# Chunked delta rule inside a four-mixer decoder trunk: values' products moved into the recurrence, panel chunks moved out of it

## What is computed

```python
def step(state, inp):
    qd, kd, uu, ww, aqk, gl = inp
    v_new = uu - jnp.einsum('bhcd,bhde->bhce', ww, state)
    o = jnp.einsum('bhcd,bhde->bhce', qd, state) + jnp.einsum('bhce,bhef->bhcf', aqk, v_new)
    state = state * gl[..., None, None] + jnp.einsum('bhcd,bhce->bhde', kd, v_new)
    return state, o
```

## Time and profile before

| | us |
|---|---|
| median of 3 runs | 2355.43 |
| lowest and highest | 2352.8, 2355.49 |
| the profiled execution's own time | 2352.03 |
| its span, first to last instruction | 2350.3 |

### The profile page before, as it was taken

The page is one execution under the profiler, slowest core; times in us unless marked ns, Lnnn a source line. Parts: engine busy times, 40 slices in busy tenths (PEclk is TensorE's granted clock), DMA queues, the critical chain, the costliest instruction groups (busy, mean ns, idle before and its releaser), DMA issues.

```text
span 2350.3 us, 37000 instructions
## 1 busy us (share of the span) xinstructions
PE 2318.3 (99%) x14463; PEld 2013.9 (86%) x14463; DVE 1434.4 (61%) x1556; ACT 1054.0 (45%) x1354; POOL 247.3 (11%) x254
## 2 busy tenths in 40 slices
PE   8999989999999999999999999999999999999999
PEld 7898878888888888888989899887888888888887
DVE  6664557555555555568666767565755554554556
ACT  4455454434434434435544445345443443443442
POOL 0052001000000000000032322200100000000000
PEclk9999999999999999999999999999999999999999
DMA  6663456665665665665534435354656656566564
GB/s 238 194 171 121 147 199 197 197 194 183 197 193 184 196 193 184 197 207 153 183 106 139 132 109 162 106 190 144 198 195 192 186 195 192 187 194 228 188 195 136
DMA packets 236680, 417.21 MB, mean 178 GB/s; under 512 B 23761, under 2 KB 46570, under 8 KB 234986
## 3 DMA queue, kind: packets, MB, share of 16 engines
q1 hardware_dynamic: 235162, 410.73, 55.5%
q10 hardware_dynamic: 1360, 4.19, 0.5%
HBM read 412.77 MB, written 2.10 MB: 177 GB/s over the span
## 4 chain that ended last, share of the span: by engine, by line
PE 95%; DVE 2%; issue 1%; ACT 1%; DMA 1%; POOL 0%; ACTq 0%; POOLq 0%; DVEq 0%
PE quad L643 20%; PE quad L668 13%; PE quad L670 13%; PE quad L669 13%; PE quad L646 10%; PE quad L614 5%; PE quad L616 5%; PE quad L618 5%; PE quad L721 1%; PE quad L1121 1%; PE quad L885 1%; PE quad L883 1%; PE quad L884 1%; PE quad L811 1%; DMA raw<-in_w_out 1%
## 5 line engine op out<-in xcount | busy, mean ns | idle before, releaser
L1684 DVE TENSOR_TENSOR wlo<-raw,whi 128x1024 fp32r<-128x1024 f32 x760 | 984.4, 1303 | 695.5 <-ACT whi L1264 692.4
L1264 ACT ACTIVATE whi<-raw 128x1024 fp32r<-128x1024 f32 x760 | 800.6, 1058 | 885.0 <-PE quad L670 468.5
L643 PE MATMUL quad<-xs,whi 128*128 128x512 f32 x2048 | 648.4, 397 | 5.4 <-DVE xs L2005 5.0
L668 PE MATMUL quad<-whi,hh 128*128 128x512 f32 x1248 | 488.7, 392 | 1.2 <-POOL hl L2373 1.0
L670 PE MATMUL quad<-whi,hl 128*128 128x512 f32 x1248 | 485.8, 389 | 0.0
L669 PE MATMUL quad<-wlo,hh 128*128 128x512 f32 x1248 | 485.6, 389 | 0.0
L646 PEld LDWEIGHTS quad<-xs,wlo 128*128 128x128 f32 x2048 | 386.2, 189 | 90.9
L646 PE MATMUL quad<-xs,wlo 128*128 128x256 f32 x2048 | 403.3, 278 | 0.0
L643 PEld LDWEIGHTS quad<-xs,whi 128*128 128x128 f32 x2048 | 314.0, 189 | 7.1 <-issue 5.8
L668 PEld LDWEIGHTS quad<-whi,hh 128*128 128x128 f32 x1248 | 234.3, 188 | 49.7 <-POOL hl L2373 1.4
L670 PEld LDWEIGHTS quad<-whi,hl 128*128 128x128 f32 x1248 | 234.2, 188 | 49.3
(11 more groups left out here) (325 smaller groups left out, 2112.5 us busy)
## 6 DMA issues: line engine op xcount, KB each, us to landing
raw<-in_mlp_w SPq DMA_DIRECT2D x512, 512.0 KB
raw<-in_gdn_w_in SPq DMA_DIRECT2D x105, 512.0 KB
raw<-in_w_out SPq DMA_DIRECT2D x64, 512.0 KB
raw<-in_mem_w_kv SPq DMA_DIRECT2D x32, 512.0 KB
raw<-in_mla_w_in SPq DMA_DIRECT2D x25, 512.0 KB
raw<-in_mla_w_ukv SPq DMA_DIRECT2D x24, 256.0 KB
gb<-in_ln_g SPq DMA_DIRECT2D x4, 1024.0 KB, 7.3
gb<-in_ln_b SPq DMA_DIRECT2D x4, 1024.0 KB, 9.4
```

Source lines behind the costliest of these rows:

```text
L643: last = nc.tensor.matmul(both, b.whi[:, slot, k, cols], b.xs[:, :, kt, :], start=start, stop=stop, skip_group_check=True)
L668: nc.tensor.matmul(ps[:, t, 0:n], ah[:, kt, toks], hi[:, k, 0:n], start=start, stop=False)
L1264: nc.scalar.activation(b.whi[:, c % NSPLIT], b.raw[:, slot], ACT.Copy).then_inc(sem.hi_ready, 1)
L1684: nc.vector.tensor_tensor(b.wlo[:, c % NSPLIT], b.raw[:, c % NRAW], b.whi[:, c % NSPLIT].bitcast(F32), ALU.subtract).then_inc(sem.lo_ready, 1)
```

## The change

- The values' product is no longer made for both halves ahead of the recurrence and copied to `uu`. A new function `new_values(g, j)` makes it for one chunk: four matmuls of 64x64 weights by 128 columns, written to those rows of the chunk's own bank in which L1185's correction comes to lie. For j = 0 it stands ahead of the keys' product; for j > 0 behind the previous chunk's output product, with `start=True`, and the state's product then accumulates onto it with `start=False`. The buffer `uu` and the signals `p_u` and `d_u` go.
- `vn` is now a plain copy from the bank: its first half on DVE, its second half (for j > 0) on ACT, with a signal of its own, `a_vn`. For j = 0 DVE copies both halves.
- The three `beside` calls inside the recurrence go; the seven chunks with indices 9 to 15 now follow it in a row. The `feed` calls inside the recurrence on ACT (three) and DVE (two) move behind it.
- The keys' products of the two chunk halves change banks, ACT copies those of the odd chunks first, and the first state increment goes to `side_ps[1]`, since the banks are needed by the accumulating products.
- PE begins chunk 0 without waiting for ACT's `wq` copies. ACT copies chunk j-1's output after its half of chunk j's `vn`.

```diff
 def out_half(j, upper):
-    c = j % 2 if j == 0 else 1 - j % 2
-    return half_rows(1 - c if upper else c)
+    return half_rows(j % 2 if upper else 1 - j % 2)
+
+def new_half(j, upper):
+    return half_rows(1 - j % 2 if upper else j % 2)
...
+            def state_bank(j):
+                return turn_ps[1] if j else side_ps[1]
...
                 for t in tiles:
                     pe.wait_ge(sem.d_xt, (g + 1) * (LEVELS - 1) * TT - TT + t + 1)
                     pe.wait_ge(sem.kd_set, g + 1)
+                    if t == 0:
+                        new_values(g, 0, True).then_inc(sem.p_vn, 1)
                     for h in range(GH):
                         for c in range(2):
                             r = slice(CHUNK * c, CHUNK * (c + 1))
-                            last = nc.tensor.matmul(turn_ps[c][:, (t * GH + h) * CHUNK:(t * GH + h + 1) * CHUNK], b.kb[r, t, h, :],
+                            last = nc.tensor.matmul(turn_ps[1 - c][:, (t * GH + h) * CHUNK:(t * GH + h + 1) * CHUNK], b.kb[r, t, h, :],
                                                     b.xt[r, t, h, :], start=t == 0 and h == 0, stop=True, skip_group_check=True)
                     last.then_inc(sem.p_w, 1)
-                    for h in range(GH):
-                        for c in range(2):
-                            r = slice(CHUNK * c, CHUNK * (c + 1))
-                            last = nc.tensor.matmul(side_ps[t][r, h * P:(h + 1) * P], b.xt[r, t, h, :], b.vr[r, t, h, :],
-                                                    start=h == 0, stop=True, skip_group_check=True)
-                    last.then_inc(sem.p_u, 1)
-                for t in tiles:
-                    pe.wait_ge(sem.a_w, n0 + t + 1)
                 for j in range(NC):
...
                     if j:
+                        pe.wait_ge(sem.a_w, n0 + 1)
+                        if j == 2:
+                            pe.wait_ge(sem.d_s, g * (NC - 1) + 1)
+                        if j == NC - 1:
+                            pe.wait_ge(sem.a_o, g * NC + 1)
+                        new_values(g, j, False)
                         pe.wait_ge(sem.d_s, g * (NC - 1) + j)
                         if j == 2:
-                            pe.wait_ge(sem.d_u, n0 + 2)
-                        if j == NC - 1:
-                            pe.wait_ge(sem.a_o, g * NC + 1)
+                            pe.wait_ge(sem.a_w, n0 + 2)
                         each(lambda h, o, s_: nc.tensor.matmul(o, b.wq[:, t, h, 2 * c:2 * c + 2, :].rearrange("p a i -> p (a i)"),
-                                                               state[:, h, :], start=s_, stop=False, skip_group_check=True),
+                                                               state[:, h, :], start=False, stop=False, skip_group_check=True),
                              bank, sem.p_vn)
-                        beside(g, LEAD + LEVELS - 2 + j)
                     pe.wait_ge(sem.d_vn, m + 1)
+                    if j:
+                        pe.wait_ge(sem.a_vn, g * (NC - 1) + j)
+                    if j == 1:
+                        pe.wait_ge(sem.a_w, n0 + 2)
...
-                beside(g, LEAD + LEVELS - 2 + NC, 2 * PANEL - (LEAD + LEVELS - 2 + NC))
+                beside(g, LEAD + LEVELS - 1, 2 * PANEL - (LEAD + LEVELS - 1))
...
+            def new_values(g, j, alone):
+                t, r = j // 2, half_rows(j % 2)
+                for h in (0, 2, 1, 3):
+                    last = nc.tensor.matmul(chunk_bank(j)[new_half(j, h >= 2), h * P:(h + 1) * P], b.xt[r, t, h, :],
+                                            b.vr[r, t, h, :], start=h % 2 == 0, stop=alone, skip_group_check=True)
+                return last
...
-                for c in range(2):
-                    ws = turn_ps[c][:, :].rearrange("p (t h i) -> p t h i", t=TT, h=GH)
+                for c in (1, 0):
+                    ws = turn_ps[1 - c][:, :].rearrange("p (t h i) -> p t h i", t=TT, h=GH)
...
+                for j in range(1, NC):
+                    act.wait_ge(sem.p_vn, g * NC + j + 1)
+                    nc.scalar.activation(b.vn[half_rows(j % 2), 0, 2:4].rearrange("p h c -> p (h c)"),
+                                         chunk_bank(j)[new_half(j, True), S:2 * S], ACT.Copy).then_inc(sem.a_vn, 1)
+                    rows_from(j - 1)
+                rows_from(NC - 1)
+                feed(8)
...
                 for j in range(NC):
                     r = slice(CHUNK * (j % 2), CHUNK * (j % 2 + 1))
-                    if j:
-                        dve.wait_ge(sem.p_vn, g * (NC - 1) + j)
-                        if j != 3:
-                            dve.wait_ge(sem.d_u, n0 + t + 1)
-                        for k in range(2):
-                            rows = half_rows(j % 2 if k == 0 else 1 - j % 2)
-                            last = nc.vector.tensor_tensor(b.vn[r, 0, 2 * k:2 * k + 2].rearrange("p h c -> p (h c)"),
-                                                           chunk_bank(j)[rows, k * S:(k + 1) * S],
-                                                           b.uu[r, t, 2 * k:2 * k + 2].rearrange("p h c -> p (h c)"), ALU.add)
-                        last.then_inc(sem.d_vn, 1)
+                    dve.wait_ge(sem.p_vn, g * NC + j + 1)
+                    for k in range(1 if j else 2):
+                        last = nc.vector.tensor_copy(b.vn[r, 0, 2 * k:2 * k + 2].rearrange("p h c -> p (h c)"),
+                                                     chunk_bank(j)[new_half(j, k == 1), k * S:(k + 1) * S])
+                    last.then_inc(sem.d_vn, 1)
```

More of the change, by code:

```diff
@@ L237, in place @@
     b.qt, _ = at("qt", [P, GH, S], F32, o)
-    b.uu, o = at("uu", quad, F32, o)
+    o += TT * GH * P * 4
     b.wq, o = at("wq", [P, TT, GH, 4, CHUNK], F32, o)
@@ L400, in __init__ @@
         self.a_w = signal("a_w")
-        self.p_u = signal("p_u")
-        self.d_u = signal("d_u")
         self.p_vn = signal("p_vn")
         self.d_vn = signal("d_vn")
+        self.a_vn = signal("a_vn")
         self.p_ds = signal("p_ds")
@@ L1195, in gdn @@
                     for h in (0, 2, 1, 3):
                         last = nc.tensor.matmul(bank[out_half(j, h >= 2), h * P:(h + 1) * P], b.aq[r, t, h, :], b.vn[r, 0, h, :],
-                                                start=j == 0 and h % 2 == 0, stop=True, skip_group_check=True)
+                                                start=False, stop=True, skip_group_check=True)
                     last.then_inc(sem.p_o, 1)
-                beside(g, LEAD + LEVELS - 2 + NC, 2 * PANEL - (LEAD + LEVELS - 2 + NC))
+                beside(g, LEAD + LEVELS - 1, 2 * PANEL - (LEAD + LEVELS - 1))
@@ L1623, in gdn, with rows_from @@
                 z_rows(g)
-                for j in range(NC):
-                    if j:
-                        feed(1)
-                    r = slice(CHUNK * (j % 2), CHUNK * (j % 2 + 1))
+                def rows_from(j):
                     act.wait_ge(sem.p_o, g * NC + j + 1)
                     for k in range(2):
-                        last = nc.scalar.activation(b.orow[r, j // 2, 2 * k:2 * k + 2].rearrange("p h c -> p (h c)"),
+                        last = nc.scalar.activation(b.orow[half_rows(j % 2), j // 2, 2 * k:2 * k + 2].rearrange("p h c -> p (h c)"),
                                                     chunk_bank(j)[out_half(j, k == 1), k * S:(k + 1) * S], ACT.Copy)
                     last.then_inc(sem.a_o, 1)
-                feed(5)
+                for j in range(1, NC):
[5 more added lines that the diff above has]
+                feed(8)
                 if g == HG - 1:
@@ L2245, in gdn @@
                     feed(1)
-                dve.wait_ge(sem.p_u, n0 + 1)
-                nc.vector.tensor_copy(b.vn[0:CHUNK, 0].rearrange("p h c -> p (h c)"),
-                                      side_ps[0][0:CHUNK, :]).then_inc(sem.d_vn, 1)
-                for t in range(TT):
-                    dve.wait_ge(sem.p_u, n0 + t + 1)
-                    nc.vector.tensor_copy(b.uu[:, t].rearrange("p h c -> p (h c)"), side_ps[t][:, :]).then_inc(sem.d_u, 1)
                 for j in range(NC):
-                    t = j // 2
                     r = slice(CHUNK * (j % 2), CHUNK * (j % 2 + 1))
-                    if j:
-                        dve.wait_ge(sem.p_vn, g * (NC - 1) + j)
-                        if j != 3:
-                            dve.wait_ge(sem.d_u, n0 + t + 1)
-                        for k in range(2):
-                            rows = half_rows(j % 2 if k == 0 else 1 - j % 2)
-                            last = nc.vector.tensor_tensor(b.vn[r, 0, 2 * k:2 * k + 2].rearrange("p h c -> p (h c)"),
-                                                           chunk_bank(j)[rows, k * S:(k + 1) * S],
-                                                           b.uu[r, t, 2 * k:2 * k + 2].rearrange("p h c -> p (h c)"), ALU.add)
-                        last.then_inc(sem.d_vn, 1)
+                    dve.wait_ge(sem.p_vn, g * NC + j + 1)
```

(4 more changed lines are left out.)

8 lines of the change are left out of this document (1 added, 7 removed).

## The result

The changed kernel took 2360.9 us (median of 20 runs, 2353.44 to 2370.05) against 2355.43; the ratio is 1.0023, 95% interval 1.0016 to 1.003. It is slower by about 5.5 us, just beyond what a measurement of this kernel tells from no change, and inside the range given. The most likely case (+1.3 us, no change that can be told) did not come; what came is a part of rival 3, which had been given 4%. Two executions of the kernel before were far slower, at 3291.65 us here and at 2548.98 us (mean clock 0.848) beside the experiments; no reading rests on them.

The account below looks back on a forecast made before the run. PE's queue, busy 99%, was taken to bound the kernel. Per group 0.51 + 2.08 + 11.40 + 0.59 = 14.58 us against 13.63, less 0.51 for chunks: +0.44, +1.3 in all, 2356.7 us; range 2352.5 to 2362.

Parts of the forecast that it names:

- The most likely case: Whole kernel: +1.3 us, 2356.7 us, no change that can be told; the forecast itself had 59%.
- rival 3: PE's granted clock falls in the recurrences, with three idle pieces of 0.8 us each: +10 us, about 2367 us; chance 4%.
- rival 1: DVE's and ACT's reads of one bank for `vn` go one after the other: total +4.7 us, 2360.1 us; chance 12%.
- The start: Chunk 0: `new_values` 0.51 us and keys' products 2.08 us, then the first increment without a wait.
- A step: Increment to increment in the recurrence: 2.10 us to the state's product plus 1.70 us, 3.80 us; low end -0.16 us.
- rival 4: Shorter steps, with `vn` copies at half their time and `new_values` free: total -1.9 us, 2353.5 us; chance 14%.
- The wait for `vn`: State's product to next increment: 1.70 us, some 0.8 us of it idle, nine times; ACT level to 0.1 us for chunk 1.
- The chunk steps: ACT's and DVE's steps moved behind the recurrence stay hidden: index 12 split 2.3 us after it, wanted 8.8 us after.
- The sum: Recurrence per group: 14.58 us after against 13.63 before, +0.95, less 0.51 for the chunks: +0.44 us, +1.3 in all.
- rival 2: `new_values` is slow in one row half, 1.08 us instead of 0.51, twelve times: total +8.1 us, 2363.5 us; chance 4%.

Follow-up runs that it names:

- e_products: The changed kernel with one panel chunk back in each step on PE, ACT's and DVE's chunk steps still behind the recurrence; 2363.09 us, ratio 1.0035.
- e_idle_work: The changed kernel with six useless matmuls in each of the nine waits for `vn`; 2355.29 us, ratio 1.0002 to the kernel before.
- e_products2: The changed kernel with one panel chunk back in each step and ACT's and DVE's chunk steps back inside the recurrence; 2347.67 us, ratio 0.9971.
- e_chunks_out: The kernel before with only its chunks and ACT's and DVE's chunk steps moved behind the recurrence; 2380.23 us, ratio 1.0096.
- e_nv_late: The changed kernel with chunks and their steps back inside, and the values' product behind the wait for the state; 2354.72 us, ratio 1.0001.
- e_fill2: The changed kernel with six of the next chunk's 24 matmuls in the second wait for `vn` of each recurrence; 2354.27 us, ratio 0.9998.

## Why the prediction was right and wrong

- *What bounds the kernel.* Right: PE's queue. What I did not weigh enough is that PE's own speed hangs on what stands in its queue. The earlier trace rows had shown a fall behind a wait of 3.19 us, and I argued that the new waits are four times shorter. The step that failed is rival 3's "the waits are four times shorter than that of rows 10. 4%": the waits, of 0.94, 0.56 and 0.56 us, stand three in 15 us among products that use a half or a quarter of the array, and that was enough for the granted clock to fall to 0.50. It should have been the first rival: the change takes the chunks out of the recurrence and leaves it the state's product, four matmuls a step, as its only work with the full array.
- *Its price.* Given as 3.4 us per recurrence (its two terms, 2 us and about as much again, make 4) and +10 us in all. Measured 2.6 and 5.3 us where it fell, but not in every recurrence: +5.5 us in the median, up to +15 in the slowest of the 20 runs.
- *The range.* That 2360.9 us lies inside it is luck: its upper end is rival 1's time plus 2 us, and rival 1 is refuted; rival 3's own time, 2367 us, stood outside.
- *The start.* Right: no wait ahead of the first increment; 2.41 us from L1214 to L1198 (2.59 forecast).
- *A step.* Output product and `new_values` were put at 1.02 us one behind the other; they run side by side, so the state's wait still ends last (L1189, 0.17 us) and increment to state's product is 1.90 us, not 2.10: the low end of the step, rival 4's half. I had looked at whether `new_values` suffers from staying in one row half, and missed that it takes the other row half than the output product next to it. The Trainium skill (page "TensorE: Matmul & The Clock Gate", section "The mechanism") says that weight loads overlap running matmuls only if the row group differs. The 0.03 us between the records of L1201 and L1214 agree with it. It would not have been enough to foretell the time, since the eight matmuls of L1168 switch the row half too and took 1.02 us.
- *The wait for `vn`.* State's product to increment 1.72 us for chunks 2 and 3 (1.70 forecast), 2.10 for chunk 1. There ACT came 0.43 us late, not level: its `wq` copies began at 1231.19 (0.22 us after PE had gone on to the increment, where I had 0.05), the state's product began 0.2 us sooner than forecast, and ACT went on 1.08 us after the tanh's start, where I had 0.96.
- *The chunk steps* hidden (the split of index 12 was done 3.2 us behind the recurrence, 2.3 forecast), the chunks behind 2.88 us apart, POOL in time: right. e_products shows what that cover is worth: 3.2 us per group when it fails.
- *The sum.* The chain alone: 14.25 against 14.58 us, so +0.1 us per group instead of +0.44. e_idle_work, with the clock held, measures it: ratio 1.0002. In it two larger terms cancel: the products' move alone is worth -7 us (e_products2), and the bare waits take as much back; what the changed kernel lies above e_idle_work, 5 to 8 us, is the clock.
- *Rival 1* is refuted by the two copies of chunk 2; *rival 2* by L1214's own 0.65 us.

Shown: that keeping PE busy in the waits takes the loss away while their ends stay within 0.1 us (e_idle_work against the changed kernel), and that the loss comes from the half of the change that takes out the chunks (e_products2, which differs from the changed kernel in the chunks and their steps alone; e_chunks_out). Not separated: whether the idle time or the small products let the clock fall. That filling waits helps speaks for the idle time, the fall of e_nv_late, with no wait over 0.3 us, for the products. Open: why some runs of the changed kernel have no fall, and why in its three traces group 0 kept the clock and groups 1 and 2 lost it, with the same instructions in the recurrence of all three.

## What to carry to other kernels

Work taken out of a chain of small matmuls can cost more than the wait it leaves, since it may be what holds TensorE's clock; before moving it, look at how much full-size work remains within the stretch, compare the mean clock of many runs, and read the granted clock of the stretch in the trace, since a short fall does not show in the mean. Where waits would stand bare, fill them, the first one first: a quarter of a chunk was enough here, and even useless matmuls paid. Two products of 64x64 weights in opposite row halves can be worth queueing next to each other, since here the second was nearly free; L1168, whose matmuls also switch the half, shows that it is not always so.

## What the runs showed of the hardware

- The granted clock fell with no wait over 0.94 us in the recurrence, and once (e_nv_late) with none over 0.3 us, behind 5 us of products with 64-row weights. In group 2 it came back 4.4 us after the first full-size chunk had begun (1510.15 to 1514.6); in e_fill2, with six full-size matmuls right behind the fall, it was back after 3.5 us.
- A run with long falls shows them in the mean clock: each 0.001 is some 2.4 us here (2353 us at 0.997, 2370 at 0.990). A short one is lost in it: the run of e_fill2 with a fall of 3.5 us has 0.996, like runs without.
- The matmuls of two products with 64x64 weights in opposite row halves alternated 0.03 us apart, eight matmuls in 0.7 us, though queued one product behind the other; eight of L1168, also switching the row half, took 1.02 us.
- DVE and ACT reading halves of one bank at once did not slow each other: 0.42 and 0.38 us.
